# Ten of the twelve modulation vectors of a two-layer diffusion backbone are computed inside the attention stage, from raw fp32 weights

## The chip, the cores and the metric

The kernel runs on one core of a Trainium2 chip. Times are device microseconds of one execution. The kernel before took 2993.22 us, the median of three runs.

## What is computed

Two layers process 640 tokens of width 1024: 512 latent tokens and 128 context tokens. Each layer is modulated by six vectors of width 1024 (shift, scale and gate for each of its two halves), once for the latent and once for the context tokens, so there are 12 vectors of two rows each:

```python
mod_ctx = (silu(c_ctx) @ w_mod[l] + b_mod[l])          # w_mod[l]: 1024 x 6144, fp32
mod_lat = (silu(c) @ w_mod[l] + b_mod[l])
shift1, scale1, gate1, shift2, scale2, gate2 = split(mod, 6)
h = rms_norm(x, g_norm1) * (1 + scale1) + shift1
x = x + gate1 * token_mixing(h)                        # four mixers A, B, C, D, gates, output projection
h = rms_norm(x, g_norm2) * (1 + scale2) + shift2
x = x + gate2 * expert_choice_ffn(h)                   # 16 experts of 1024 x 1024 x 3
```

The results must agree with fp32 arithmetic closely enough for the router's choice of tokens, which is why all large products are made of three fp32r products (below).

## The kernel before, in words

It is written engine by engine, with semaphores and with the order of the work laid out by hand and by small planners at the top of the file.

**The ring.** SP (L502 to L608) fills a ring of weight chunks of 512 KB, in attention and in the modulation stage of 8 slots, in the expert stage of 16 (the slots beyond 8 lie over the attention's memory). ACT copies a chunk to `high` (fp32r, `split_high`, L1013), DVE makes `low` as the difference (`split_low`, L1325), and PE multiplies `high` and `low` (`three`, L464 to L468: high*high, low*high, high*low). `split_high` runs four chunks ahead of PE. A slot is refilled when PE has used its chunk (`ring_used`).

**The modulation stage** comes first. The 12 vectors (q = 0 to 11) are made one after another: 8 chunks of `w_mod` each (96 chunks, 50 MB), multiplied by the split pair of silu(c), silu(c_ctx) (`mod_rows`, L630), evacuated with the bias (`mod_evac`, L1364), high and low part summed by a small product with `pair_sum` (`mod_tail`, L646), evacuated with the gain (`mod_copy`, L1375) and stored in DRAM by ACT (`mod_store`, L1045). POOL loads the vectors from DRAM, broadcast to 128 partitions, where they are used (`mod_in`, L1783, and L1883, L1898, L1899). The first vectors' load (gain and shift of layer 0) is done while the stage still runs.

**A layer.** The norm (`stats`, L1399; PE turns it at L621), the projections of mixer D and of A (tiles of 128 tokens, all four chunks of a piece per tile, `dense_tile`), then the attention in 82 steps, one for each of 80 units (head, block of queries) and two to drain. In a step PE makes the scores of unit ui (L809), work of slot 0, the transposes of the probabilities of unit ui-1 (`turn`, L827), work of slot 1, the values of unit ui-2 (`values`, L837), work of slot 2. The work in the slots is written in the table `AT` by `plan_steps` (L128): the remaining projections (W), the gates (G) and the branch products (B), in pieces of one token tile by one chunk, and the transposes of the next heads. It fills PE between the steps of the softmax, in which DVE and ACT have their turns. After attention come the output projection, the second norm, the router, and 16 experts.

**Banks.** All work of the slots writes one of two PSUM banks, 5 and 7. `plan_uses` (L164) gives each use the bank that the use before it did not have, and while a tile is open (its four chunks not yet done) everything else goes to the other bank. `bank_free` (L682) lets PE wait until ACT or DVE has read what was in the bank before (`tile_out`, L1092, with L1101 for W and the tanh at L1109 for G; `gate_mul` for B, L1513).

## Time and profile before

| what | value |
|---|---|
| three runs | 2998.76, 2993.22, 2990.93 us |
| the profiled execution's own time | 2989.55 us |
| its span, first to last instruction | 2987.6 us |
| PE, DVE, ACT, POOL busy | 90%, 67%, 53%, 15% of the span |
| chain of work that ended last | PE 77%, DVE 10%, issue 5%, ACT 5%, DMA 2% |
| DMA | 593.80 MB, 199 GB/s on average |

The span falls into stages: modulation up to about 184 us, then for each layer norm and first projections, attention (285 to 868 us, and 1670 to 2256 us), output projection with norm and router, and experts. In a row of the profile an engine's busy time is that of its instructions. Matmuls overlap, so the spacing of their starts is the price of one, and the printed mean duration is more than that. A wait in brackets behind a row is the engine's idle time just before it, with what ended it. One fp32 matmul (not fp32r) leaves two records of MATMUL.

### The profile page before, as it was taken

Reading aid. Unit: us, or ns where it says so; the run is one execution under the profiler, and the core shown is the slowest. Engines: PE = TensorE matmul, PEld = TensorE weight load, DVE = VectorE, ACT = ScalarE, POOL = GpSimd, SP = SyncE. Lnnn points to the kernel's source line nnn. Section 1 sums busy time; section 2 is a strip of 40 time slices with the busy share of each in tenths; the row PEclk is TensorE's granted clock in tenths of the full one; section 3 lists DMA queues with packets and bytes.
Section 4 is the critical chain, followed back from the end, with each engine's and each line's share of the span. In section 5 each row is a group of like instructions: output and inputs, shape, how many; then the busy total and the mean of one; then the engine's idle time right before and its main releaser. Section 6 shows DMA issues by size and latency. Waiting matters only on the chain.

```text
span 2987.6 us, 40730 instructions
## 1 busy us (share of the span) xinstructions
PE 2686.8 (90%) x13616; PEld 1916.9 (64%) x13616; DVE 1987.8 (67%) x3069; ACT 1575.4 (53%) x2278; POOL 462.2 (15%) x335
## 2 busy tenths in 40 slices
PE   6779999999996699999988999999999499999994
PEld 1248777777775466666657777777777366666662
DVE  7864356535336799999975346643434699999994
ACT  5643344334323577777753444433422387777773
POOL 0003000212130112112211200031122112211201
PEclk8989999999998899999998999999999699999997
DMA  9942012112144699999983211121134399999994
GB/s 333 333 144 89 29 37 60 50 44 63 67 157 148 231 375 380 381 377 378 381 283 107 73 33 36 36 71 43 43 113 153 113 361 380 382 376 382 381 382 145
DMA packets 190521, 593.80 MB, mean 199 GB/s; under 512 B 22945, under 2 KB 32991, under 8 KB 190391
## 3 DMA queue, kind: packets, MB, share of 16 engines
q1 hardware_dynamic: 171638, 527.66, 48.0%
q0 software_dynamic: 18640, 64.20, 7.4%
q8 instruction: 79, 1.29, 0.2%
q14 instruction: 52, 0.42, 0.0%
q10 hardware_dynamic: 112, 0.23, 0.0%
HBM read 566.78 MB, written 25.23 MB: 198 GB/s over the span
## 4 chain that ended last, share of the span: by engine, by line
PE 77%; DVE 10%; issue 5%; ACT 5%; DMA 2%; ACTq 0%; SPq 0%; POOL 0%; DVEq 0%; POOLq 0%
PE bank L466 21%; PE bank L468 20%; PE bank L467 20%; PE bank L837 4%; PE bank L809 4%; DVE low L1329 2%; ACT high L1023 2%; PE bank L827 2%; PE bank L641 1%; PE bank L640 1%; DMA ring<-in_w_mod 1%; DVE st L1583 1%; PE bank L949 1%; PE bank L981 1%; DVE sigr L1513 1%
## 5 line engine op out<-in xcount | busy, mean ns | idle before, releaser
L1023 ACT ACTIVATE high<-ring 128x1024 fp32r<-128x1024 f32 (+1 forms) x1008 | 1053.8, 1052 | 447.0 <-PE bank L468 369.1
L1736 DVE TENSOR_TENSOR low<-ring,high 128x1024 fp32r<-128x1024 f32 x736 | 880.4, 1220 | 72.7 <-ACT high L1023 70.9
L466 PE MATMUL bank<-high,hT_high 128*128 128x512 f32 (+2 forms) x1280 | 520.9, 407 | 25.2 <-ACT sigr L1109 13.6
L467 PE MATMUL bank<-low,hT_high 128*128 128x512 f32 (+2 forms) x1280 | 485.4, 379 | 0.0
L468 PE MATMUL bank<-high,hT_low 128*128 128x512 f32 (+2 forms) x1280 | 484.2, 378 | 0.0
L1329 DVE TENSOR_TENSOR low<-ring,high 128x1024 fp32r<-128x1024 f32 (+2 forms) x272 | 321.8, 1210 | 138.7 <-ACT high L1023 137.7
L466 PE MATMUL bank<-high,xeT_high 128*80 128x512 f32 x1024 | 406.1, 397 | 2.1 <-DVE xeT_low L1334 2.1
L468 PE MATMUL bank<-high,xeT_low 128*80 128x512 f32 x1024 | 403.9, 394 | 0.0
L467 PE MATMUL bank<-low,xeT_high 128*80 128x512 f32 x1024 | 403.6, 394 | 0.0
L1210 ACT ACTIVATE att<-bank,st 128x640 f32<-128x640 f32 (+3 forms) x200 | 136.7, 684 | 351.2 <-DVE st L1588 256.5
L466 PEld LDWEIGHTS bank<-high,hT_high 128*128 128x128 f32 x1280 | 243.7, 190 | 78.4 <-ACT sigr L1109 18.2
L468 PEld LDWEIGHTS bank<-high,hT_low 128*128 128x128 f32 x1280 | 242.7, 190 | 47.4
L467 PEld LDWEIGHTS bank<-low,hT_high 128*128 128x128 f32 x1280 | 244.3, 191 | 32.5
L1583 DVE TENSOR_REDUCE st<-bank 128x1 f32<-128x640 f32 (+3 forms) x200 | 136.6, 683 | 116.6 <-PE bank L809 114.4
L466 PE MATMUL bank<-high,hidT_high 128*80 128x512 f32 x512 | 203.9, 398 | 10.6 <-DVE hidT_low L1334 8.9
L468 PEld LDWEIGHTS bank<-high,xeT_low 128*80 128x80 f32 x1024 | 151.8, 148 | 84.7 <-issue 0.7
L466 PEld LDWEIGHTS bank<-high,xeT_high 128*80 128x80 f32 x1024 | 151.9, 148 | 83.4 <-DVE xeT_low L1334 2.6
L467 PEld LDWEIGHTS bank<-low,xeT_high 128*80 128x80 f32 x1024 | 152.3, 149 | 80.4 <-issue 0.7
L468 PE MATMUL bank<-high,hidT_low 128*80 128x512 f32 x512 | 202.8, 396 | 0.0
L467 PE MATMUL bank<-low,hidT_high 128*80 128x512 f32 x512 | 202.7, 396 | 0.0
L1923 POOL DMA_INDIRECT x_resid<-oTr,idx_s x32 | 91.5, 2860 | 686.2 <-DVE oTr L1699 667.2
L1914 POOL DMA_INDIRECT U<-x_normed,idx_g x32 | 132.1, 4129 | 327.3 <-issue 104.2
(237 smaller groups left out, 3298.6 us busy)
## 6 DMA issues: line engine op xcount, KB each, us to landing
ring<-in_w_e_gate SPq DMA_DIRECT2D x256, 512.0 KB, 6.2
ring<-in_w_e_up SPq DMA_DIRECT2D x256, 512.0 KB, 6.9
ring<-in_w_e_down SPq DMA_DIRECT2D x256, 512.0 KB, 6.4
ring<-in_w_mod SPq DMA_DIRECT2D x96, 512.0 KB, 6.0
ring<-in_w_gate SPq DMA_DIRECT2D x64, 512.0 KB, 3.9
ring<-in_w_in SPq DMA_DIRECT2D x24, 512.0 KB, 4.5
ring<-in_w_branch SPq DMA_DIRECT2D x16, 512.0 KB, 4.2
ring<-in_w_out SPq DMA_DIRECT2D x16, 512.0 KB, 4.8
```

Source lines behind the costliest of these rows:

```text
L466: nc.tensor.matmul(out, lhs[0], rhs_high, start=start, stop=False)
L467: nc.tensor.matmul(out, lhs[0], rhs_low, start=False, stop=False)
L468: return nc.tensor.matmul(out, lhs[1], rhs_high, start=False, stop=stop)
L809: ins = mm(ps[p % 2][:, col:col + w], qT[r0:r0 + rn, b, un["m"] * P:(un["m"] + 1) * P], kT[r0:r0 + rn, b, a:a + w], start=True, stop=True)
L837: ins = mm(bank(6, P, P + HD), probT[:, ui % 2, i * P:(i + 1) * P], v_src(un, kb), start=(i == 0), stop=(i == len(un["kb"]) - 1))
L1023: A(high[:, HSLOT[g], :, 0:w], ring[:, SLOT[g], :, 0:w], ACT.Copy).then_inc(high_done, 1)
L1210: A(prob[:, p % 4, 0:w], ps[p % 2][:, 0:w], ACT.Exp, bias=negm[:, p % 8:p % 8 + 1], scale=SCALE[un["br"]], accum_out=sm[:, p % 8:p % 8 + 1 ...
L1329: V.tensor_tensor(low[:, SLOT[g], :, 0:w], ring[:, SLOT[g], :, 0:w], high[:, HSLOT[g], :, 0:w].bitcast(F32), ALU.subtract).then_inc(low_dv ...
L1583: then(V.tensor_reduce(mx[:, c8:c8 + 1], S[:, 0:w], AX.X, ALU.max))
L1736: V.tensor_tensor(low[:, SLOT[ahead], :, :], ring[:, SLOT[ahead], :, :], high[:, HSLOT[ahead], :, :].bitcast(F32), ALU.subtract).then_inc( ...
L1914: pool.indirect_dma_start(out=xe[0:CAP, b, :], out_offset=None, in_=xn_dram, in_offset=bass.IndirectOffsetOnAxis(ap=idx_g[:, b, 0:1], axis ...
L1923: pool.indirect_dma_start(out=x_dram, out_offset=bass.IndirectOffsetOnAxis(ap=idx_s[:, e, 0:1], axis=0), in_=ybuf[0:CAP, e, :], in_offset= ...
```

## The change

Only vectors 0 and 1 (shift and scale of layer 0's first half) are made in the modulation stage, now of 16 chunks. The other ten are made in attention, six in layer 0's and four in layer 1's. Each is cut into four quarters of 256 columns: 24 products in layer 0, 16 in layer 1. A product (`mod_product`) is eight fp32 matmuls on PE, silu(c) and silu(c_ctx) as two stationary columns and raw fp32 weights as the moving operand, no splitting. It stands in slot 1 of the steps 8 + 68*i//24 and takes a bank by the planner's rule. SP brings a quarter's weights (1 MB, four DMAs of 256 KB) into ring slots 6 and 7 once the product before it is done; attention's chunks have slots 0 to 5. ACT copies the two rows out of PSUM (`sum_out`), POOL stores them in DRAM; once a vector's quarters are there POOL loads it with the bias (and gain) as 64 partitions by 16 for either group, adds and multiplies, and stores it again (`raw_store`, `fin_load`, `fin_store`).

```diff
-N_MOD = 6 * D // NW
-CH_MOD = NQ * N_MOD * L
+RING_D = 6
+CH_MOD = 2 * KD
+MOD_COLS = 256
+MOD_ROWS = 2
+VECTORS = [[(0, 2), (0, 3), (0, 4), (0, 5), (1, 0), (1, 1)], [(1, 2), (1, 3), (1, 4), (1, 5)]]
+SUMS = [[(lv, v, a) for lv, v in vs for a in range(D // MOD_COLS)] for vs in VECTORS]
+SUM0 = [0, len(SUMS[0]), len(SUMS[0]) + len(SUMS[1])]
+N_PIECE = KD // MOD_ROWS
+def sum_step(i):
+    return 8 + 68 * i // len(SUMS[0])
...
     # plan_steps
+    for i in range(len(SUMS[0])):
+        at[sum_step(i)][1].append(("sum", i))
...
     # plan_uses
+        if x[0] == "sum":
+            freed[r] = ("sum", x[1])
+            continue
...
     # plan_ring
-        a, h = (SLOT_E[e % RING_E], e % HIGH_E) if e >= 0 else (g % RING, g % HIGH)
+        a, h = (SLOT_E[e % RING_E], e % HIGH_E) if e >= 0 else (g % RING if g < CH_MOD else (g - CH_MOD) % CH_LAYER % RING_D, g % HIGH)
...
+        mod_w = ring[:, RING_D:RING_D + 2, :, :].rearrange("p s h (k n) -> p (s h) k n", k=MOD_ROWS)
...
     # SP
+                mods = [(sum_step(i - 1) if i else -1, N_PIECE * (SUM0[l] + i) + k) for i in range(len(SUMS[l])) for k in range(N_PIECE)]
+                def mod_fills(step):
+                    while mods and mods[0][0] < step:
+                        nn = mods.pop(0)[1]
+                        i, k = divmod(nn, N_PIECE)
+                        lv, v, a = (SUMS[0] + SUMS[1])[i]
+                        if nn == N_PIECE * SUM0[l]:
+                            sp.wait_ge(ring_used, chunk_no(l, 0))
+                        if i and k == 0:
+                            sp.wait_ge(sum_full, i)
+                        src = w_mod[lv].rearrange("(k p) n -> p k n", p=P)[:, MOD_ROWS * k:MOD_ROWS * (k + 1),
+                                                                          v * D + a * MOD_COLS:v * D + (a + 1) * MOD_COLS]
+                        sp.dma_start(mod_w[:, k, :, :], src).then_inc(mod_w_in[k], 16)
...
                     for kq in range(chunks):
                         g = chunk_no(l, n)
+                        mod_fills(RELEASE_STEP[n])
                         fill(g, w_chunk(w, n0, width, kq), width)
...
     # PE
-            for q in range(L * 6):
+            for q in range(2):
                 mod_rows(q)
                 if q:
                     mod_tail(q - 1)
...
+                def mod_product(i):
+                    if i < len(SUMS[l]):
+                        n, r = SUM0[l] + i, USE["sum", i]
+                        bank_free(r)
+                        for k in range(KD):
+                            if k % MOD_ROWS == 0:
+                                pe.wait_ge(mod_w_in[k // MOD_ROWS], 16 * (n + 1))
+                            ins = mm(bank_use(r, 0, MOD_COLS)[0:2, :], csf[:, k, :], mod_w[:, k // MOD_ROWS, k % MOD_ROWS, :],
+                                     start=(k == 0), stop=(k == KD - 1))
+                        ins.then_inc(sum_full, 1)
...
     # ACT
-            for q in range(L * 6):
-                if q + 1 < L * 6:
-                    if q:
-                        act.wait_ge(mod_row, q)
-                    bias_in(q + 1)
...
+            bias_in(1)
+            for g in range(HIGH, CH_MOD + HIGH):
+                split_high(g)
+            for q in range(2):
                 mod_store(q)
...
+                def sum_out(i):
+                    if i < len(SUMS[l]):
+                        n = SUM0[l] + i
+                        act.wait_ge(sum_full, n + 1)
+                        if n:
+                            act.wait_ge(raw_out, 16 * n)
+                        A(mod_row2[:, :], bank_use(USE["sum", i], 0, MOD_COLS)[0:2, :], ACT.Copy).then_inc(sum_ev, 1)
...
     # POOL
+            def raw_store(i):
+                lv, v, a = (SUMS[0] + SUMS[1])[i]
+                pool.wait_ge(sum_ev, i + 1)
+                if i:
+                    pool.wait_ge(raw_out, 16 * i)
+                pool.dma_start(raw_dram[lv, :, v * D + a * MOD_COLS:v * D + (a + 1) * MOD_COLS], mod_row2[:, :]).then_inc(raw_out, 16)
...
+                for i in range(len(SUMS[l])):
+                    n = SUM0[l] + i
+                    mod_work.append((sum_step(i) + 1.5, raw_store, (n,)))
+                    if i % N_PIECE == N_PIECE - 1:
+                        mod_work.append((sum_step(i) + 2.5, fin_load, (VEC0[l] + i // N_PIECE, n)))
+                        mod_work.append((sum_step(i) + 3.5, fin_store, (VEC0[l] + i // N_PIECE,)))
```

**How the order moves, on SP.** These are SP's fills from the first attention chunks on, before:

```order
L516 DMA ring<-in_w_in 128x2x512 [waits ring_used] x4
L516 DMA ring<-in_w_gate 128x2x512 [waits ring_used] x4
L516 DMA ring<-in_w_branch 128x2x512 [waits ring_used]
L516 DMA ring<-in_w_gate 128x2x512 [waits ring_used] x4
L516 DMA ring<-in_w_branch 128x2x512 [waits ring_used]
```

and with the change, at the same place:

```order
L547 DMA ring<-in_w_in 128x2x512 [waits ring_used] x2
L603 DMA ring<-in_w_mod 128x2x256 [waits ring_used]
L603 DMA ring<-in_w_mod 128x2x256 x3
L547 DMA ring<-in_w_in 128x2x512 [waits ring_used] x2
L547 DMA ring<-in_w_gate 128x2x512 [waits ring_used] x2
L603 DMA ring<-in_w_mod 128x2x256 [waits sum_full]
L603 DMA ring<-in_w_mod 128x2x256 x3
L603 DMA ring<-in_w_mod 128x2x256 [waits sum_full]
L603 DMA ring<-in_w_mod 128x2x256 x3
```

SP now waits for products (`sum_full`) between the waits for chunks (`ring_used`), and four DMAs of raw weights stand behind each such wait.

**How the order moves, on PE.** This is layer 0's attention, step 42, where the first tile of mixer C's projection ends and the second begins. `bank2` holds bank 5, `bank3` bank 7; L837 are the values (in the other half of bank 6). Before:

```order
L837 MATMUL bank3<-U,att 128x64 x4
L466 MATMUL bank3<-high_51,hT_high 128x512
L467 MATMUL bank3<-low_50,hT_high 128x512
L468 MATMUL bank3<-high_51,hT_low 128x512
L466 MATMUL bank3<-high_51,hT_high 128x512
L467 MATMUL bank3<-low_50,hT_high 128x512
L468 MATMUL bank3<-high_51,hT_low 128x512
L466 MATMUL bank2<-high_51,hT_high 128x512
L467 MATMUL bank2<-low_50,hT_high 128x512
L468 MATMUL bank2<-high_51,hT_low 128x512
```

With the change:

```order
L918 MATMUL bank3<-ring_49,csf 2x256 x8
L893 MATMUL bank3<-att 128x64
L893 MATMUL bank3<-U,att 128x64 x4
L497 MATMUL bank2<-high_51,hT_high 128x512
L498 MATMUL bank2<-low_50,hT_high 128x512
L499 MATMUL bank2<-high_51,hT_low 128x512
L497 MATMUL bank2<-high_51,hT_high 128x512
L498 MATMUL bank2<-low_50,hT_high 128x512
L499 MATMUL bank2<-high_51,hT_low 128x512
L497 MATMUL bank2<-high_51,hT_high 128x512
L498 MATMUL bank2<-low_50,hT_high 128x512
L499 MATMUL bank2<-high_51,hT_low 128x512
```

Before, the second tile begins in the other bank; with the product (L918) inside the first tile, the second tile begins in the bank that the first has just left.

## Rows read from the trace of the kernel before

**Rows 1.** Busy time by stage (us, busy and count per engine, PEclk, DMA share, GB/s).

```profile
core 0: us, PE busy (x) PEld busy (x) DVE busy (x) ACT busy (x) POOL busy (x), PEclk, DMA share, GB/s
0.00:184.00 184.00, 134.20 (x428) 35.09 (x428) 143.97 (x148) 102.28 (x104) 5.07 (x13) 0.88 0.92 329
...
285.00:868.00 583.00, 549.55 (x3115) 440.81 (x3116) 273.27 (x656) 222.89 (x463) 73.77 (x61) 1.00 0.18 57
...
1670.00:2256.00 586.00, 553.52 (x3131) 443.84 (x3129) 274.99 (x658) 224.00 (x463) 74.71 (x61) 0.99 0.18 56
```

**Rows 2.** Timeline, PE and DVE at the end of vectors 1 and 11, norm.

```profile
28.99 0.62 PE L641 MATMUL bank<-high,csT 128*4 128x512 f32 x2
...
45.62 1.27 DVE L1371 TENSOR_TENSOR U<-bank,U 4x512 f32<-4x512 f32 x2
...
164.21 0.40 PE L641 MATMUL bank<-high,csT 128*4 128x512 f32 x1
...
183.59 1.27 DVE L1371 TENSOR_TENSOR U<-bank,U 4x512 f32<-4x512 f32 x2
...
188.52 1.28 DVE L1387 COPY U<-bank 2x512 f32<-2x512 f32 x2 [2.47 <-PE bank L652]
...
193.21 1.28 DVE L1418 SCALAR_TENSOR_TENSOR att<-att,st,M 128x1024 f32<-128x1024 f32 x1
```

**Rows 3.** Timeline, store of vector 1 by ACT, and POOL's load behind it.

```profile
61.14 0.24 ACTq L1048 DMA_DIRECT2D mod_rows<-U  x1
66.29 0.53 POOL L1787 DMA_DIRECT2D M<-mod_rows  x1 [56.08 <-DMA mod_rows<-U]
```

**Rows 4.** The same load's line: time to landing.

```profile
DMA to landing us min/median/max: 5.0/6.4/10.7
```

**Rows 5.** Timeline, PE, fp32 products before attention and in the modulation stage.

```profile
43.22 1.87 PE L652 MATMUL bank<-U,pair_sum 4*2 4x512 f32 x4
...
277.90 2.75 PE L760 MATMUL bank<-M 128*128 128x256 f32 x12
```

**Rows 6.** Timeline, PE, change from fp32 scores to fp32r chunks.

```profile
286.47 0.36 PE L466 MATMUL bank<-high,hT_high 128*128 128x256 f32 x1
286.67 0.28 PE L467 MATMUL bank<-low,hT_high 128*128 128x256 f32 x1
286.79 0.28 PE L468 MATMUL bank<-high,hT_low 128*128 128x256 f32 x1
```

**Rows 7.** What PE waited for, 285 to 868 us (first six of twelve).

```profile
PE bank L837 <- issue: 7.7, 11, 1.6
PE bank L466 <- ACT sigr L1109: 7.4, 8, 1.4
PE bank L809 <- ACT att L1178: 4.9, 8, 1.3
PE bank L809 <- ACT att L1175: 2.5, 2, 1.6
PE bank L851 <- DVE oT_low L1521: 2.5, 3, 1.6
PE bank L466 <- ACT U L1101: 2.4, 2, 1.7
```

**Rows 8.** Timeline, PE, tiles behind a tile in the same bank.

```profile
411.56 0.50 PE L466 MATMUL bank<-high,hT_high 128*128 128x512 f32 x1 [1.29 <-ACT sigr L1109]
443.91 0.50 PE L466 MATMUL bank<-high,hT_high 128*128 128x512 f32 x1 [1.41 <-ACT sigr L1109]
698.09 0.50 PE L466 MATMUL bank<-high,hT_high 128*128 128x512 f32 x1 [1.00 <-ACT sigr L1109]
```

**Rows 9.** Timeline, PE, a values group that waited in a step that gets a product.

```profile
352.26 0.96 PE L837 MATMUL bank<-M,att 128*128 128x64 f32 x7 [0.43 <-issue]
```

**Rows 10.** DMA issues: KB each, median us to landing.

```profile
ring<-in_w_in SPq DMA_DIRECT2D x24, 512.0 KB, 4.5
ring<-in_w_in SPq DMA_DIRECT2D x16, 256.0 KB, 3.2
```

**Rows 11.** The page's costliest groups: busy, mean ns, idle before.

```profile
L1023 ACT ACTIVATE high<-ring 128x1024 fp32r<-128x1024 f32 (+1 forms) x1008 | 1053.8, 1052 | 447.0 <-PE bank L468 369.1
...
L1329 DVE TENSOR_TENSOR low<-ring,high 128x1024 fp32r<-128x1024 f32 (+2 forms) x272 | 321.8, 1210 | 138.7 <-ACT high L1023 137.7
```

**Rows 12.** Timeline, PE in the modulation stage behind a wait, and without one.

```profile
36.81 0.58 PE L640 MATMUL bank<-low,csT 128*2 128x512 f32 x1 [2.78 <-DVE low L1329]
37.20 0.63 PE L641 MATMUL bank<-high,csT 128*4 128x512 f32 x1
37.62 0.63 PE L640 MATMUL bank<-low,csT 128*2 128x512 f32 x1
...
160.34 0.39 PE L641 MATMUL bank<-high,csT 128*4 128x512 f32 x1
160.57 0.40 PE L640 MATMUL bank<-low,csT 128*2 128x512 f32 x1
```

**Rows 13.** Timeline, POOL, mixer C's rotation and its wait in the middle.

```profile
559.05 1.27 POOL L1774 TENSOR_TENSOR U<-U,rope 128x192 f32<-128x192 f32 x2 [161.61 <-PE bank L851]
...
570.77 1.61 POOL L1843 DMA_DIRECT2D att<-rpb_padded  x2 [8.29 <-DVE st L1588]
```

More of the change, by code:

```diff
@@ L205 @@
 USE, USE_BANK, BEFORE, FREED, FULL, N_USE, LOWS_AFTER, LOWS_END = plan_uses()
+STEP_OF = {x: i for i, step in enumerate(AT) for slot in step for x in slot}
+RELEASE_STEP = [-1] * RING_D + [STEP_OF.get(("dense", pc, T - 1, kq), -1 if pc[0] == "W" else 2 * N_UNIT)
+                                for pc in STREAM for kq in range(CHUNKS_IN[pc])] + [2 * N_UNIT] * (2 * NQ)
 def count_of(*key):
@@ L269, in hybrid_step @@
         mod_dram = nc.dram_tensor("mod_rows", (L, 2, 6 * D), F32, kind="Internal").ap()
+        raw_dram = nc.dram_tensor("mod_raw", (L, 2, 6 * D), F32, kind="Internal").ap()
         rpb_dram = nc.dram_tensor("rpb_padded", (L, HEADS * 15, 127), F32, kind="Internal").ap()
@@ L398, in hybrid_step @@
         g_row_in = sem("g_row_in")
+        mod_w_in = [sem(f"mod_w_in{i}") for i in range(N_PIECE)]
+        sum_full, sum_ev, raw_out = sem("sum_full"), sem("sum_ev"), sem("raw_out")
+        fin_in, fin_out = sem("fin_in"), sem("fin_out")
         eps_set, sq_done = sem("eps_set"), sem("sq_done")
@@ L585, in matrix @@
                             sp.wait_ge(o_ev, N_UNIT * (l + 1))
+                        if i is None and SLOT[g + k] == RING_D:
+                            sp.wait_ge(raw_out, 16 * SUM0[l + 1])
                         if i is None and SLOT[g + k] == 13:
@@ L658, in _ @@
                     mod_tail(q - 1)
-            mod_tail(L * 6 - 1)
-            pe.wait_ge(sum_ready, L * 6)
+            mod_tail(1)
+            pe.wait_ge(sum_ready, 2)
             for l in range(L):
@@ L682, in bank_free @@
                 def bank_free(r):
-                    if BEFORE[r] is not None:
-                        by, n = FREED[BEFORE[r]]
-                        if by == "act":
+                    r = BEFORE[r]
+                    while r is not None and FREED[r][0] == "sum" and FREED[r][1] >= len(SUMS[l]):
+                        r = BEFORE[r]
+                    if r is not None:
+                        by, n = FREED[r]
+                        if by == "sum":
+                            pe.wait_ge(sum_ev, SUM0[l] + n + 1)
+                        elif by == "act":
                             pe.wait_ge(tile_act, N_USE["act"] * l + n)
@@ L857, in between @@
                             dense(*x)
+                        elif what == "sum":
+                            mod_product(*x)
                         elif what == "prep":
@@ L1053, in _ @@
                 split_high(g)
-            for q in range(L * 6):
-                if q + 1 < L * 6:
-                    if q:
-                        act.wait_ge(mod_row, q)
-                    bias_in(q + 1)
-                if q >= 2:
-                    mod_store(q - 2)
-                if q % 3 == 0 and q:
-                    gain_row_in(q + 1)
-                for k in range(KD):
-                    split_high(KD * q + k + HIGH)
-            for q in range(L * 6 - 2, L * 6):
+            bias_in(1)
+            for g in range(HIGH, CH_MOD + HIGH):
+                split_high(g)
+            for q in range(2):
                 mod_store(q)
@@ L1193, in between @@
                             prep_out(*x)
+                        elif what == "sum":
+                            sum_out(*x)
                         elif what == "oT":
                             turn_o_high(*x)
-                        elif x[0] == 2:
+                        elif what == "on" and x[0] == 2:
                             act.wait_ge(on_var, l + 1)
@@ L1391, in _ @@
                 split_low(g)
-            for q in range(L * 6):
+            for q in range(2):
                 for k in range(KD):
@@ L1804, in _ @@
                         mod_in(q1, g)
-                    for b in range(2):
-                        pool.wait_ge(mod_out[b], 16 * 3 * L)
                 def rope_rows(X, t0, tmp, heads, d4):
@@ L1819, in tile_done, with mod_until @@
                     pool.wait_ge(tile_act, N_USE["act"] * l + count_of("dense", pc, m))
+                mod_work = []
+                for i in range(len(SUMS[l])):
[4 more added lines that the diff above has]
+                        mod_work.append((sum_step(i) + 3.5, fin_store, (VEC0[l] + i // N_PIECE,)))
+                mod_work.sort(key=lambda w: w[0])
+                def mod_until(step):
+                    while mod_work and mod_work[0][0] < step:
+                        _, work, args = mod_work.pop(0)
+                        work(*args)
                 flat = lambda t: t[0, l].rearrange("t h n -> t (h n)")
```

50 lines of the change are left out of this document (43 added, 7 removed).

## The prediction

> **What bounds the kernel now.** I read the busy time by stage first, because a change that moves work from one stage to another is worth the difference of two prices. In the modulation stage (the first 184 us) the DMA engines are busy 0.92 of the time, while PE works 134 of 184 us; in both attention stages it is the other way round: DMA 0.18, PE 550 of 583 us and 554 of 586 us [rows 1]. So the stage that is shortened is bound by weights coming in (and by their splitting), and the stage that receives the work is bound by PE. Next I read the timeline around the ends of vectors, to see what a vector costs and what follows the last one [rows 2 to 4]; then the spacing of fp32 records, the price of a product [rows 5]; then what PE waits for in attention, to see how much room there is [rows 7].
>
> **The sum, part by part.** It is made against the profiled execution (2989.55 us, span 2987.6 us), which lies 3.7 us under the median of the three runs, 2993.2 us; differences are added to that median.
>
> *The modulation stage gets shorter.* Before, the last bias addition (vector 11) starts at 183.59 us and the norm's first multiplication at 193.21 us [rows 2]. With the change the order at the end of the stage is the same (last chunk of `w_mod`, 17 small loads, four chunks for mixer D whose lows DVE makes before it evacuates the last vector), only that the last fill is that of chunk 15. It waits for chunk 7's product: PE ends it at about 29.3 us instead of 164.6 us for chunk 87 [rows 2]. From there to the last evacuation took 183.59 - 164.6 = 19.0 us, so now 48.3 us. From the evacuation to the end of the last copy it is 189.8 - 183.6 = 6.2 us [rows 2]: 54.5 us. Now comes something that was hidden before: the norm needs gain and shift, which POOL loads only when both vectors are stored. ACT issued that store at 61.14 us, and POOL saw it at 66.29 us: 5.1 us, with the DMA engines full [rows 3]; they are empty now, so 3 to 5 us. The load itself takes 5.0 us at least and 6.4 us at the median [rows 4], behind a second issue of 0.5 us [rows 3]. Sum: 54.5 + 4 + 0.5 + 5.7 = 64.7 us, against 193.2: **-128.5 us** (bounds -125 and -131).
>
> *The products.* The nearest rows are the fp32 products of 256 columns before attention: 12 records in 2.75 us, of which some 0.17 us is the last one's tail, hence 0.213 us each; and four records of 512 columns over two stationary columns in 1.87 us, 0.427 us each [rows 5]. So width of the stationary side does not matter, and 0.213 us is the price. A product has 8 matmuls, 16 records: 3.41 us. 40 of them: **+136.5 us**, and PE has nothing better to do in their place only where it waits. *By the Trainium skill ("TensorE: Matmul & The Clock Gate", section on the back-to-back issue gap) a stream of load and matmul pairs sustains about 81 ns for 128 columns and 131 ns for 512; between them, an estimate of 98 ns a pass for 256, and the products would be 125 us. The rows show 107 ns a pass, two to a record, and they decide.*
>
> *Changing over.* Behind fp32 work the first fp32r matmul of a chunk holds the second off by 0.20 us where the next ones follow by 0.12 us [rows 6]. One such change for each product: 40 x 0.08 = +3 us.
>
> *Banks.* A product inside an open tile takes the other bank, and the next tile then gets the bank that the open tile is just leaving, so PE must wait for ACT's reading; a product behind a closed tile can itself land on a bank not yet read. Walking through the two orders, I count nine places in layer 0 and nine in layer 1, net of one that goes, in which a use now stands directly behind the reader of its bank. Such a place costs PE 1.0 to 1.4 us [rows 8], less where other work lies between: 1.0 us each, **+18 us**. Bounds: nothing, where ACT reads at once and scores lie between, and 18 x 1.4 = 25 us.
>
> *Waits that the products fill.* PE's visible idle time in attention is 583 - 550 = 33 us and 32 us [rows 1]. Only waits in the product's own step shrink. The product stands between turn and values, so the values no longer wait for ACT's copy of the transposes: 0.43 us in such a step [rows 9], four such steps a layer. The waits for ACT's sigmoid and exponentials in the list [rows 7] stand mostly in other steps, or are of the kind that the bank rule makes. I take -3 us a layer, **-6 us**; bounds: none, and a third of all idle time, -22 us.
>
> *Six ring slots instead of eight.* The third and fourth chunk of a projection are now asked for only when the first two chunks of the piece before are used, in a stretch where all four are needed for the first tile. They take 3.2 us (256 KB) and 4.5 us (512 KB) to land [rows 10] and then 1.05 us on ACT and 1.2 us on DVE [rows 11]. Following the times of the first projections of A, that is 0.3 us for the query piece and 1.1 us for the key and value piece, in both layers, and up to 0.5 us in the output projection: **+4 us**; bounds 0 and 10. In attention itself two uses of chunks lie about 5.5 us apart, which covers 4.5 us.
>
> *At no cost.* ACT's 40 small copies: ACT is busy 223 of 583 us [rows 1]; without that cover they would cost PE the bank time above again. SP's 160 DMAs: 1 MB per product over at least 16 us, on DMA engines that are busy 0.18. SP's new wait stands ahead of a chunk's fill, but always for a product of an earlier step than the release of that chunk's slot. POOL's 106 DMAs of about 0.53 us [rows 3] are 56 us on an engine that is busy 74 us of each 583. The expert stage reads 16 slots as before.
>
> Sum: -128.5 + 136.5 + 3 + 18 - 6 + 4 = **+27 us**, so 2993 + 27 = **3020 us**. The expected gain is there, and PE gives it back where it has no time to spare.
>
> **The rivals.**
>
> *A: PE's idle time swallows more.* If the products, wherever they stand, let ACT and DVE catch up so that a third of the 65 us of idle time goes, and the bank waits are covered too: -128.5 + 136.5 + 3 - 22 + 4 = -7, so **2986 us**, near no change. For it: most waits are short and of one kind, PE a little ahead of ACT [rows 7]. Against it: a wait behind a tile in the same bank comes back after each product, and the steps without a product (58 of 82 in layer 0) keep theirs.
>
> *B, the one on the other side: faster.* The mechanism is attention's slack: PE runs ahead until the softmax chain of a step (reduction, exponential, turn) is late, so a product in a step whose chain is later than PE costs nothing. It decides from the point where more than 17 us beyond the bank waits is swallowed. With two thirds of the idle time gone, -128.5 + 136.5 + 3 - 43 + 4 = -28: **2965 us**. Against it: idle time is only 6% of attention, and a step lasts some 7 us, of which the product takes half again.
>
> *C: POOL is late, and ACT with it.* ACT may copy a product's rows only when POOL has stored the ones before. In the middle of mixer B's first heads POOL is held by a wait for DVE of 8.3 us and then rotates mixer C's tiles [rows 13]; the store of the product of step 44 stands behind two of them. If ACT waits there, PE's next bank is late too: 3 to 10 us a layer on top, **3033 us**.
>
> *D: PE's clock falls.* In attention the granted clock is 1.00 [rows 1]. In the modulation stage it was lower: after a wait of 2.8 us, records of 512 columns stood 0.42 us apart (the 1.2 GHz level), in a stretch without such a wait 0.23 us (2.4 GHz) [rows 12]. What went before the fall was idle time, and the products bring none. If the clock did fall for each product, it would cost 3.4 us more apiece: 3020 + 136 = **3156 us**. [...]
>
> **How the numbers follow.** My forecast gets 0.62, A 0.20, B 0.06, C 0.09, D 0.03. A measurement of this kernel can tell about 0.3%, 9 us, from no change. A lies at -7 and spreads to both sides of that bound: 0.03 faster, 0.15 the same, 0.02 slower. The forecast's own range, from its bounds, is 3004 to 3040, with 0.02 in the band. So faster 0.09, same 0.17, slower 0.74. The range takes in most of A and C: 2988 to 3042 us leaves out B, D and the ends of A and C, some 0.2.
>
> **What the changed profile should show.** The norm's first multiplication (L1418 before) at 65 us. Products as groups of 16 records of 3.6 us with the tail, PEclk 1.00 around them. Attention 583 us before, some 673 us in layer 0, and 586 us before, some 648 us in layer 1. More waits of PE for ACT's sigmoid, about 8 us a layer. Nearly no wait of PE for the raw weights. Wrong would be: attention longer by clearly less than 3.4 us per product (A or B), ACT waiting for a DMA of POOL (C), PEclk under 0.95 in attention (D), or a start of the norm beyond 70 us.

## The result, and the profile after

The changed kernel takes 3031.8 us (median of 4 runs, 3029.3 to 3034.3) against 2994.7 us for the kernel before on the same chip: ratio 1.0124, 95% interval 1.0106 to 1.0141. It is slower by 37 us; 27 us were forecast. The profiled execution took 3034.3 us with a span of 3032.5 us, 44.9 us above the span of before (2987.6 us); the two profiles lie at opposite ends of their runs. Each variant below was timed beside the kernel before, not all of them on one chip, so two variants are compared by their ratios to it; a single profile can lie 8 us from the median of its kernel's runs.

First the busy time by stage, the answer to [rows 1] (us, busy time and count per engine, PEclk, DMA share, GB/s):

```profile
core 0: us, PE busy (x) PEld busy (x) DVE busy (x) ACT busy (x) POOL busy (x), PEclk, DMA share, GB/s
0.00:155.80 155.80, 114.17 (x536) 81.26 (x536) 82.02 (x149) 62.33 (x110) 26.98 (x50) 0.88 0.45 154
155.80:841.50 685.70, 647.58 (x3501) 476.83 (x3502) 274.23 (x656) 231.82 (x485) 108.47 (x137) 0.98 0.27 84
...
1648.00:2298.50 650.50, 613.36 (x3373) 463.22 (x3374) 274.40 (x656) 228.70 (x477) 96.46 (x111) 0.99 0.24 75
```

The three windows shown end at the first scores of layer 0, at the first transposes behind its attention, and at the end of layer 1's attention; the third begins at layer 1's first scores. Read in the same way, the stages moved so (us; the middle row is what lies between the two attentions, the last what follows the second):

| stage | before | after | difference | forecast |
|---|---|---|---|---|
| start to first scores | 285.4 | 155.8 | -129.6 | -128.5 and a part of the ring's +4 |
| attention, layer 0 | 583.2 | 685.7 | +102.5 | +90 |
| to the first scores of layer 1 | 800.5 | 806.5 | +6.0 | part of the ring's +4 |
| attention, layer 1 | 585.2 | 650.5 | +65.3 | +62 |
| the rest | 733.3 | 734.0 | +0.7 | 0 |

PE is busy for almost all of attention, as before; its idle time there is 38.1 and 37.1 us (33.5 and 32.5 us in [rows 1]). So most of what was added is PE's own work, and most of the excess over the forecast lies in layer 0. The clock is 0.98 there, not 1.00 (0.99 in layer 1).

The end of the modulation stage on the timeline, the answer to [rows 2, 3]:

```profile
47.89 1.27 DVE L1444 TENSOR_TENSOR U<-bank,U 4x512 f32<-4x512 f32 x2
...
50.39 3.98 ACTq L1118 DMA_DIRECT2D mod_rows<-U  x2
...
56.02 0.53 POOL L1896 DMA_DIRECT2D M<-mod_rows  x1 [46.32 <-DMA mod_rows<-U]
...
61.77 1.28 DVE L1492 SCALAR_TENSOR_TENSOR att<-att,st,M 128x1024 f32<-128x1024 f32 x1 [4.28 <-DMA oTr<-mod_rows]
```

The last bias addition stands at 47.89 us (48.3 forecast), and the norm's first multiplication at 61.8 us (64.7 forecast), now behind the load of gain and shift. Next one product in the stream, the answer to [rows 5, 6]:

```profile
198.13 0.71 PE L883 MATMUL bank<-ident,att 128*128 128x128 f32 x5
198.77 3.62 PE L918 MATMUL bank<-ring,csf 128*2 128x256 f32 x16
202.31 1.33 PE L893 MATMUL bank<-M,att 128*128 128x64 f32 x10
```

From the first of the 16 records to the next work it is 3.54 us, so 0.22 us a record with the change to the next work. All 40 products take 3.54 or 3.55 us: the term was 3.41 + 0.08 = 3.49 us.

### The profile page after: what moved, and what is told of

Same layout as the page of the kernel before. It is cut to its first block, busy times and chain, and to the rows that moved or that the text cites. A ratio compares the mean times of both kernels' runs of the same rounds, so it can differ in the third digit from the quotient of the medians.

```text
span 3032.5 us, 41346 instructions
## 1 busy us (share of the span) xinstructions
PE 2739.3 (90%) x13896; PEld 1946.5 (64%) x13896; DVE 1872.3 (62%) x2949; ACT 1511.2 (50%) x2238; POOL 508.2 (17%) x457
## 4 chain that ended last, share of the span: by engine, by line
PE 79%; DVE 7%; issue 5%; ACT 5%; DMA 4%; SPq 0%; POOL 0%; ACTq 0%; DVEq 0%; POOLq 0%
PE bank L497 21%; PE bank L499 19%; PE bank L498 19%; PE bank L918 5%; PE bank L893 4%; PE bank L865 4%; PE bank L883 2%; ACT high L1093 2%; DVE low L1402 1%; DMA ring<-in_w_gate 1%; DVE st L1657 1%; PE bank L672 1%; PE bank L1019 1%; DMA ring<-in_w_in 1%; PE bank L1051 1%
## 5 line engine op out<-in xcount | busy, mean ns | idle before, releaser
L1093 ACT ACTIVATE high<-ring 128x1024 fp32r<-128x1024 f32 (+1 forms) x928 | 974.2, 1052 | 425.7 <-PE bank L499 371.9
L1402 DVE TENSOR_TENSOR low<-ring,high 128x1024 fp32r<-128x1024 f32 (+2 forms) x192 | 229.0, 1206 | 127.2 <-ACT high L1093 126.4
L1682 DVE TENSOR_SCALAR U<-bank,st 128x64 f32<-128x64 f32 x120 | 34.1, 284 | 324.1 <-PE bank L893 323.3
```

Of the source, the lines that this page charges most:

```text
L1093: A(high[:, HSLOT[g], :, 0:w], ring[:, SLOT[g], :, 0:w], ACT.Copy).then_inc(high_done, 1)
L1402: V.tensor_tensor(low[:, SLOT[g], :, 0:w], ring[:, SLOT[g], :, 0:w], high[:, HSLOT[g], :, 0:w].bitcast(F32), ALU.subtract).then_inc(low_dv ...
```

## Where the unforeseen time sits

What PE waited for in layer 0's attention, and below it what ACT waited for from there to the end of the output projection (line, what it waited for, us in total, times, longest):

```profile
PE bank L497 <- ACT sigr L1171: 10.5, 10, 2.2
PE bank L865 <- ACT att L1240: 4.7, 8, 1.3
PE bank L893 <- issue: 4.2, 6, 1.5
PE bank L497 <- ACT U L1163: 3.1, 3, 1.7
...
PE bank L497 <- ACT att L1237: 2.7, 1, 2.7
...
PE bank L918 <- ACT sigr L1171: 1.4, 2, 0.7
PE bank L918 <- DVE sigr L1587: 1.1, 1, 1.1
PE bank L918 <- ACT U L1163: 0.9, 1, 0.9
```

```profile
ACT high L1093 <- DMA ring<-in_w_gate: 7.2, 5, 3.6
ACT high L1093 <- DMA ring<-in_w_out: 4.5, 4, 1.3
ACT mod_row L1250 <- DMA mod_raw<-mod_row: 3.2, 1, 3.2
ACT high L1093 <- DMA ring<-in_w_in: 1.1, 1, 1.1
```

Before the change ACT waited for no chunk of the ring in these stretches. Now it does, 12.8 us in layer 0 and 11.7 us in layer 1, more than half of it for gate weights; in the projections just ahead of the first scores it waits another 3.5 and 3.0 us. The longest such wait of layer 0 on ACT's timeline, and what PE made of it (in layer 1 it is 4.8 us on ACT and 3.4 us on PE):

```profile
792.51 1.06 ACT L1093 ACTIVATE high<-ring 128x1024 fp32r<-128x1024 f32 x1 [0.33 <-PE bank L499]
797.14 1.06 ACT L1093 ACTIVATE high<-ring 128x1024 fp32r<-128x1024 f32 x1 [3.58 <-DMA ring<-in_w_gate]
798.11 0.58 ACT L1171 ACTIVATE sigr<-bank 128x512 f32<-128x512 f32 x1
```

```profile
796.17 0.40 PE L499 MATMUL bank<-high,oT_low 128*128 128x512 f32 x1
798.74 0.57 PE L497 MATMUL bank<-high,oT_high 128*128 128x512 f32 x1 [2.17 <-ACT sigr L1171]
799.11 0.63 PE L498 MATMUL bank<-low,oT_high 128*128 128x512 f32 x1
799.53 0.63 PE L499 MATMUL bank<-high,oT_low 128*128 128x512 f32 x1
```

The wait is booked to ACT's sigmoid (L1171), because that came last. But ACT had stood idle for a transfer ahead of the split in front of that sigmoid; the line that a wait names is not its cause. A weight is asked for when the slot six chunks back is free; in the ring of eight it was asked for two chunks earlier. Behind the wait PE's records stand 0.43 us apart instead of 0.23 us until 802.5 us: the 1.2 GHz level. Five such stretches lie in layer 0: up to 160.7 us, and from 277, 287, 694 and 799 us, where before there was one (0.89 in a window of 15 us). The first three stand behind waits that the kernel before has too (1.26 us at 275.5 us, for example), the last two behind late chunks. The first three last some 12 us together, and records at that level stand about twice as far apart, so by estimate they cost 6 us, and the one before cost 2 us; why the clock fell there in this profile is not shown. In windows of 15 us, columns as above:

```profile
275.00:290.00 15.00, 12.99 (x72) 10.15 (x73) 10.79 (x24) 7.77 (x16) 1.15 (x2) 0.79 0.60 193
680.00:695.00 15.00, 11.62 (x60) 9.01 (x61) 5.90 (x12) 8.27 (x17) 2.70 (x2) 0.94 0.61 210
695.00:710.00 15.00, 14.14 (x61) 9.40 (x60) 7.23 (x15) 3.21 (x8) 6.21 (x5) 0.83 0.11 36
```

The stretch from 694 us stands behind the other late chunk: ACT stood 2.58 us for a gate chunk until 691.58 us and only then split it and made the copy for which PE waited 2.70 us.

Theory R: the ring of six slots, sized at 4 us, costs several times that, directly and through the clock. Rivals: S, the sum's sizes hold and the excess is the banks' (which the sum has at 18 us); P, it is something in the products themselves.

## The experiments

**The ring alone.** The kernel before, with this edit only:

```diff
+RING_D = 6
-        a, h = (...) if e >= 0 else (g % RING, g % HIGH)
+        a, h = (...) if e >= 0 else (g % RING if g < CH_MOD else (g - CH_MOD) % CH_LAYER % RING_D, g % HIGH)
```

> The kernel before, with only the dense stage's ring cut from 8 slots to 6 (no products in attention, the modulation stage of twelve vectors as it was). Theory R: the ring is what the prediction sized wrongly. Chunks asked for two slots later arrive late, ACT waits for them (some 13 us a layer in the changed kernel, none before), PE behind it, and its clock falls after the two longest of these waits: +20 to +28 us, about 3019 us. Theory S, the prediction's term: +4 us, about 2999 us. Theory P: the missing 10 us lie in the products and the banks, then this kernel is within 9 us of the one before and its ACT shows few waits for ring transfers.

Measured: 3005.5 us, ratio 1.0040 (1.0025 to 1.0055), so +12 us (7.5 to 16.5). Less than the 20 us of theory R; S's 4 us lie under the interval, and P, which had few waits for transfers, is contradicted by the timeline. The same late chunks of the last gates appear without any product (PE waits 2.51 us in layer 0, 3.56 us in layer 1; 0.57 us before). ACT and then PE, layer 0:

```profile
833.66 1.06 ACT L1024 ACTIVATE high<-ring 128x1024 fp32r<-128x1024 f32 x1 [3.92 <-DMA ring<-in_w_gate]
834.62 0.58 ACT L1110 ACTIVATE sigr<-bank 128x512 f32<-128x512 f32 x1
```

```profile
835.25 0.79 PE L467 MATMUL bank<-high,oT_high 128*128 128x512 f32 x1 [2.51 <-ACT sigr L1110]
835.85 0.63 PE L468 MATMUL bank<-low,oT_high 128*128 128x512 f32 x1
836.27 0.63 PE L469 MATMUL bank<-high,oT_low 128*128 128x512 f32 x1
```

Not all of it lies there. Against the profile of before, the two attentions are 6.4 and 2.9 us longer, the time to the first scores 2.9 us, and what lies between the attentions 5.7 us. That last stretch was not traced: products_alone, with eight slots, adds 1.5 us there, early_products, which gives its slots back before the stretch and takes two again at the start of layer 1, 5.6 us.

**The products alone.** The changed kernel with eight slots and a constant table in place of the raw weights, which are not loaded (so its ten vectors are not those of the computation):

```diff
-RING_D = 6
+RING_D = 8
-                        mod_fills(RELEASE_STEP[n])
-                            ins = mm(bank_use(r, 0, MOD_COLS)[0:2, :], csf[:, k, :], mod_w[...], ...)
+                            ins = mm(bank_use(r, 0, MOD_COLS)[0:2, :], csf[:, k, :], rope[...][:, 0:MOD_COLS], ...)
```

> The changed kernel with a ring of 8 slots and no transfer of raw weights: the 40 products stand where they stood, with their 16 records, but multiply a constant table of the same width, so the ten vectors are not those of the reference. Theory R: the two slots' price goes, 3032 - 25 = 3007 us (3002 to 3012), and ACT waits for no ring chunk in attention. Theory S (ring worth 4 us): 3028 us. Theory P as S.

Measured: 3017.1 us, ratio 1.0081 (1.0064 to 1.0098). The price of the two slots inside the change is the difference of the ratios, 0.0043 or 13 us, with some 7 us of uncertainty: again three times the term, and again half of R's size. Its stages:

```profile
154.70:828.40 673.70, 637.85 (x3501) 469.02 (x3502) 273.31 (x656) 231.47 (x485) 108.99 (x135) 1.00 0.16 49
...
1630.40:2278.30 647.90, 613.44 (x3374) 463.14 (x3375) 274.01 (x656) 228.84 (x477) 97.04 (x109) 0.99 0.17 51
```

Attention is 90.5 us and 62.7 us longer than before, where the forecast's steps for products, changing over, banks and filled waits gave 90 and 62. ACT waits for no ring chunk in either layer from the first scores to the end of the output projection, and PEclk is 1.00 and 0.99. P is out. In layer 0's attention this profile is 12.0 us shorter than that of the change, but half of that can be the three stretches of lower clock that stood behind no late chunk; the 13 us rest on the medians.

**Products early, the ring given back.**

```diff
 def sum_step(i):
-    return 8 + 68 * i // len(SUMS[0])
+    return 8 + i
+GROW = 30
+        if c == GROW:
+            free = [6, 7] + free
```

> The changed kernel with one product in each step from step 8 on (24 steps in layer 0, 16 in layer 1), and the ring back at 8 slots from chunk 30 of the layer on, once the last product is made. Everything is computed. Theory R: the late chunks of gates 4 to 7 and of the output projection come early again, three quarters of the ring's 25 us go: 3013 us (3008 to 3020). Theory S: 3030 us, no change that can be told. A third, C: with a product in every step POOL's stores of raw rows hold ACT up (one such wait of 3.2 us a layer in the changed kernel) and 3 to 10 us a layer come back: 3025 us or more.

Measured: 3017.4 us, ratio 1.0083 (1.0065 to 1.0101), as if the ring were whole, though everything is computed. ACT's waits for gate and output weights are gone in both layers (0.4 and 0.9 us of waits for `w_in` are left of 12.8 and 11.7 us), and C did not appear: ACT waits for no store of POOL. So most of the ring's price is paid by the chunks of the second half, as the timeline said; that the products' own places moved too was not separated.

**Products at tile edges.** Each product moved to the next place where a tile begins.

```diff
-        at[sum_step(i)][1].append(("sum", i))
+        s, j, k = min(... for ... if (s, j) >= (want, 1) and x[0] == "dense" and x[3] == 0)
+        at[s][j].insert(k, ("sum", i))
```

> The changed kernel with each product moved by up to two and a half steps so that it stands between two tiles instead of inside an open one; ring, transfers and number of products as in the change. The tile behind it then finds its bank's reader done 3.5 us earlier. The bank term of the prediction was +18 us; the traces of the changed kernel show the waits for ACT's and DVE's reading of tiles only 8 us longer in both layers together. If those 8 us go and nothing else changes: 3032 - 8 = 3024 us (3020 to 3028). If the bank order costs more than its visible waits (with the clock that falls behind them): 3014 to 3020 us. If it costs nothing (the waits only moved): 3032 us.

Measured: 3044.0 us, ratio 1.0153 (1.0134 to 1.0172): 9 us slower than the change, with some 8 us of uncertainty, which no theory expected. It does not speak on the banks, since the move ran into something else. ACT, and PE behind it:

```profile
499.52 0.37 ACT L1257 ACTIVATE mod_row<-bank 2x256 f32<-2x256 f32 x1 [17.98 <-DMA mod_raw<-mod_row]
```

```profile
499.94 0.80 PE L504 MATMUL bank<-high,hT_high 128*128 128x512 f32 x1 [6.32 <-ACT mod_row L1257]
500.54 0.63 PE L505 MATMUL bank<-low,hT_high 128*128 128x512 f32 x1
```

This is rival C of the prediction, at its place: POOL waited 11.8 us for DVE, rotated a tile of mixer C, and only then stored the rows that ACT's copy was waiting for; the same again in layer 1 (6.54 us on PE). In the changed kernel that wait is there too, 3.2 and 3.1 us of ACT, and PE does not feel it.

**The banks, without that.** The order is changed in two ways: the tile behind a product takes the product's bank, and each product is moved by at most a step and a slot.

```diff
-            at[r] = 1 - at[r - 1] if open_at is None and r else (1 - open_at if r else 0)
+            at[r] = 1 - turn_at if open_at is None and r else (1 - open_at if r else 0)
+            if x[0] != "sum" or open_at is None:
+                turn_at = at[r]
```

> The changed kernel with two edits in the order alone: the tile behind a product that stood inside an open tile takes the product's bank, not the one that is just being left; and each product is moved by up to a step and a slot to where its own bank has been read for 1.5 us. By the order, the places where a use stands directly behind the reader of its bank fall from 32 and 36 (layer 0, layer 1) to 24 and 22, as before the change (24 and 24). Ring, transfers, number and price of the products stay. If the bank term is what the waits of the changed kernel show, 8 us: 3024 us (3020 to 3028). If it is the prediction's 18 us: 3014 us. If bank waits only move (as at_tile_edges, which mixed them with a wait for POOL's stores, could not exclude): 3032 us.

Measured: 3019.9 us, ratio 1.0075 (1.0062 to 1.0088). Against the change that is 0.0049, 15 us, with some 7 us of uncertainty; 8 us and 18 us are both inside. Its stages:

```profile
154.85:828.50 673.65, 638.45 (x3501) 472.33 (x3502) 273.83 (x656) 232.49 (x485) 110.82 (x137) 0.99 0.27 86
1632.90:2276.20 643.30, 610.24 (x3374) 463.46 (x3375) 274.25 (x656) 229.48 (x477) 98.48 (x111) 0.99 0.24 76
```

Attention is 12.0 and 7.2 us shorter than in the change, though ACT waits for gate chunks as long as there (14.0 and 13.8 us over the run). Of these 19 us, 7 are idle time of PE and 12 are busy time, at a slightly higher clock; but this profile is the fastest of its five runs and that of the change the slowest of its four, and two low stretches of the change behind waits of before are not in it. That bank waits cost more than they show as waits (some 8 us in both layers), by the clock behind them, is therefore likely and not shown; the term of 18 us is neither confirmed nor refined.

**Both cures.** early_products with the banks edit and its own table of places.

> early_products with the edits of banks_kept: one product in each step from step 8 on, the ring back at 8 slots behind the last, the tile behind a product in the product's bank, each product at the best slot of its step. Everything is computed, all 16 records of a product stay. Theory: the ring's price (15 us by early_products) and the banks' (12 us by banks_kept) are separate: 3032 - 27 = 3005 us (3000 to 3010), so the products alone keep the kernel slower than before. Rival: with a product in every step the places behind a reader stay 31 and 32, against 24 before, and the gain of banks_kept does not come: 3014 to 3018 us.

Measured: 3031.5 us, ratio 1.0121 (1.0102 to 1.014): by the ratios 11 us slower than early_products alone, with some 8 us of uncertainty, and both the sum and the rival missed. The waits for banks did go (5.5 + 4.1 us ahead of products and tiles up to 480 us in early_products, here 1.4 us), but the places were less than a step apart in parts, and four products of layer 0 wait for their weights, for example

```profile
304.96 5.30 PE L942 MATMUL bank<-ring,csf 128*2 128x256 f32 x16 [2.12 <-DMA ring<-in_w_mod]
```

9.7 us together, and three more in layer 1, 7.1 us; behind each wait the product runs at the lower clock for a part: these rows show 5.3 to 6.4 us where others show 3.6. Whether the two cures add when spaced well was not tried.

**The weighting on DVE.** What is left of the excess is the price of 16 records. Here DVE multiplies and adds the eight rows for both vectors, and PE only adds over the partitions (4 records), with the ring whole again from chunk 54:

```diff
-                        for k in range(KD):
-                            ... mm(bank_use(r, 0, MOD_COLS)[0:2, :], csf[:, k, :], mod_w[...])
+                        pe.wait_ge(acc_done, 2 * KD * (n + 1))
+                        for g in range(2):
+                            ... mm(bank_use(r, 0, MOD_COLS)[0:2, :], sel[:, g, :], acc[:, g, :])
+    # DVE
+                            V.scalar_tensor_tensor(out=acc[:, g, :], in0=raw, scalar=c1, in1=acc[:, g, :],
+                                                   op0=ALU.mult, op1=ALU.add).then_inc(acc_done, 1)
```

> The products' weighting moved to DVE: DVE multiplies and adds the eight 256-column rows of a product for both conditioning vectors (16 operations of 128x256), and PE only adds over the partitions with two matmuls, 4 records for 16. Ring back at 8 slots from chunk 54 on. Everything is computed. If PE's time in the stream is what the products cost (theory R): 40 x 12 x 0.213 = 102 us less, and some 15 us of the ring: 3032 - 117 = 2915 us. Rival: DVE becomes late. By its rows (128x128 0.29 us, 128x512 0.69 us) an operation takes 0.42 us, 6.7 us a product, 161 us in layer 0's attention on top of 274 us, and if each of the 72 steps that get some waits 1 us longer for the softmax chain, half of the gain is eaten in both layers: 2915 + 60 = 2975 us or more.

Measured: 3017.7 us, ratio 1.0080 (1.0062 to 1.0099). The rival, and more: it is no faster than the variants that keep all 16 records. PE was busy 605.5 of 676.8 us in layer 0's attention, 71 us idle, at PEclk 0.96. A third of DVE's operations stood ahead of the copy for the turn and a third ahead of the next maximum. So the next kernel had all of them right ahead of DVE's wait for the values (each product also stands up to one step later):

```diff
                         then(V.reciprocal(rinv[:, r:r + 1], sm[:, p:p + 1]))
+                        acc_ops(ui, 0)
                         dve.wait_ge(o_full, N_UNIT * l + v + 1)
```

> As sums_on_dve, but DVE's 16 operations of a product stand in one place of each step, right ahead of its wait for the values, where it sat idle 176 us in layer 0 of the changed kernel; before, a third stood ahead of the copy for the turn and a third ahead of the next step's maximum, and PE waited 71 us in layer 0's attention (37 us in early_products). Theory L (the late softmax chain ate the gain): most of these 34 us and the clock's 20 us go in layer 0, half as much in layer 1: 3017 - 60 = 2957 us, within 2950 to 2975. Rival: DVE's work as such is too much, wherever it stands: 3005 us or more.

Measured: 2992.0 us, ratio 0.9982 (0.9972 to 0.9992). By the ratios 29 us came from the place, half of what theory L gave, and not by its path: in layer 0's attention PE's idle time fell by 4 us only (71.3 to 67.3), its busy time by 15 us (605.5 to 590.4), with PEclk 0.98 in place of 0.96. Four more runs varied where the products stand.

> sums_on_dve_2 with the products at tile edges as in at_tile_edges. If the bank waits add up with the rest: 8 us less than sums_on_dve_2. Rival: the uneven distances (one to four steps between products, so 16 operations of 0.4 us in one step twice) cost that much again: no difference.

Measured: 3021.6 us, ratio 1.0074 (1.0055 to 1.0093), 28 us slower than sums_on_dve_2: worse than its rival. ACT's copy waits 25.8 us for stores of POOL over the run (up to 9.3 us at once, and PE 5.3 us behind one of them), as in at_tile_edges; what the uneven distances add was not separated.

> sums_on_dve_2 with the same two edits of the order (places chosen for a product of 1 us). In sums_on_dve_2 PE waits longest at these: six waits for ACT's reading ahead of products, 8.2 us in each layer, and 14.7 and 12.2 us ahead of tiles. Theory: bank waits go back to those before the change, some 9 us a layer less: 2992 - 18 = 2974 us (2968 to 2982), a version under the kernel before. Rival: DVE's lateness takes their place (PE waits 8 us a layer for its U and att already): 2985 us or more.

Measured: 2989.5 us, ratio 0.9972 (0.996 to 0.9985). The rival: 3 us less than sums_on_dve_2, within the noise. The waits named below took the place of the bank waits:

```profile
PE bank L541 <- ACT U L1207: 7.2, 2, 5.2
PE bank L963 <- DVE ring L1691: 5.7, 3, 2.9
```

> sums_on_dve_3 with all products in the middle slot of their step, behind the turn, where DVE's last operation for them is long done. In sums_on_dve_3 eight stood in the first slot, and PE waited 5.7 us for DVE's sums in layer 0. Theory: those waits and a part of the clock that fell behind them go: 2989 - 8 = 2981 us (2976 to 2986). Rival: no change, 2989 us.

Measured: 2958.2 us, ratio 0.9869 (0.9851 to 0.9887): **faster than the kernel before by 39 us** (34 to 45), and than the change by 76 us. The gain over sums_on_dve_3 is 31 us, not 8. The wait for DVE's sums is gone, and so is the 5.2 us behind POOL's store (1.1 us of ACT are left of it). Between the two profiles PE's idle time in the attentions fell by 13 us and its busy time by 17 us, at a higher granted clock (0.97 and 0.99, before 0.96 and 0.97); so more than half of the gain is the clock behind the waits by this reading, which no run isolates. Its stages, and a product with part of its sums:

```profile
156.40:802.30 645.90, 591.32 (x3213) 455.44 (x3214) 427.50 (x1040) 229.87 (x485) 112.64 (x137) 0.97 0.29 91
...
1607.90:2220.10 612.20, 569.41 (x3181) 446.11 (x3182) 371.63 (x912) 227.39 (x477) 101.75 (x111) 0.99 0.27 82
```

```profile
183.97 3.26 DVE L1691 SCALAR_TENSOR_TENSOR ring<-ring,csf 128x256 f32<-128x256 f32 x8
...
188.53 1.02 PE L963 MATMUL bank<-ring,sel 128*2 128x256 f32 x4
```

Eight operations take 3.26 us, 0.41 each, as estimated; DVE is busy 427 of 646 us. Both attentions are 62.7 and 27.0 us longer than before, against 102.5 and 65.3 us in the change, and the modulation stage gives 129 us.

> sums_on_dve_4 with no product between steps 42 and 47, where POOL rotates mixer C's tiles and its stores of raw rows come late; in sums_on_dve_3 PE waited 5.2 us (layer 0) and 4.6 us (layer 1) there for an ACT that stood behind such a store, at a clock that had then fallen. Theory (rival C of the prediction, in one place): 10 us less than sums_on_dve_4, some 2972 us. Rival: the same work of DVE packed into fewer steps ahead of it costs that again: no difference to sums_on_dve_4.

Measured: 2959.0 us, ratio 0.9879 (0.9863 to 0.9896): no difference to sums_on_dve_4, as the rival said, though perhaps not for its reason: the long wait had already gone with the places of sums_on_dve_4, so the detour had little left to save.

## Why the prediction was right, and where a size was off

The direction and the mechanism held: the stage bound by transfers gave 129.6 us, and PE gave it back in attention. The 10 us between 27 and 37 us are of the size that one term, the ring, was off; the terms for banks and filled waits agree only as a sum.

- **The modulation stage**, -128.5 us: -131.4 us by the norm's first multiplication, -129.6 us by the first scores. From the end of the last copy (52.82 + 1.28 = 54.1 us) to the norm it was 7.7 us, where 4 + 0.5 + 5.7 us had been put.
- **The products**, +136.5 and +3 us: 40 x 3.54 = 141.6 us, 2 us above. The row of fp32 products [rows 5] was the right price, also for two stationary columns; with the tail of 0.17 us it gives 0.215 us a record rather than the 0.213 us that was used, which is half of the 2 us. *The estimate by the rates that the Trainium skill states ("TensorE: Matmul & The Clock Gate", section on the back-to-back issue gap), 125 us, was 17 us under what this trace shows.*
- **Banks and filled waits**, +18 and -6 us. The values' waits fell from 7.7 and 7.0 us to 4.2 us in each layer, 3 us a layer as said. The waits for readers of tiles rose by some 3 and 4 us, not by 9 a layer (5.6 and 7.7 us with the waits behind late chunks); the edit that takes them away brought 15 us, with 7 us of uncertainty (banks_kept). In products_alone attention grew by what the four terms say together, to a microsecond in each layer, but that is the sum and not each term, and in part luck: PE's idle time rose by 2.8 and 2.0 us only, and the other 7 us of the 12 that banks and filled waits were given are busy time of PE beyond 40 x 3.54 us, which no run assigns.
- **Six ring slots**, +4 us, bounds 0 to 10. This is the term that was mis-sized: 12 us alone (ring6_alone, interval 7.5 to 16.5), 13 us in the change. The sentence that failed is "In attention itself two uses of chunks lie about 5.5 us apart, which covers 4.5 us". Its working looked at the projections ahead of attention (where PE waits 0.6 us a layer for lows in the change) and took an average inside it. In the steps where one piece ends and the next begins a chunk is asked for and wanted within about one transfer, three such transfers share the queues (DMA share 0.92 from 820 to 835 us in ring6_alone), and what landed in 4.5 us at the median comes 3.6 and 2.6 us late in layer 0 of the change. Ahead of one of them (the chunk at 691.6 us) SP had also issued four pieces of raw weights (2.0 us), which the prediction had listed under "At no cost". That the clock falls behind such a wait was in no term.
- **The clock**, 1.00 in the forecast's checks: 0.98 and 0.99 in the two attentions. Rival D was wrong as it was put (the products themselves run at 2.4 GHz, all 40 of them), but what it read from its row held: idle time went before the falls, and late chunks bring idle time.
- **At no cost:** PE never waited for raw weights in the change, as said. POOL's stores held ACT up 3.2 us once a layer without reaching PE (rival C); moved by a step they cost PE 6 us a layer.
- A and B are out: attention was longer by more than 3.4 us per product, not less. Idle time did not swallow the products.

The expectations of the study had two errors of their own: theory R gave the ring all that the other terms left over in one profile (20 to 28 us), while two profiles of one kernel can lie several us apart and the medians gave 12 and 13; and the three runs that moved products to save bank waits and met another wait (at_tile_edges, early_and_banks, sums_on_dve_edges) came out 20 to 38 us over what was expected. sums_on_dve_4 missed by 23 us the other way.

## What to carry to other kernels

Work that moves from a stage bound by transfers to one bound by PE gains only the difference of two prices, so price it in the receiving engine's records; here PE's price in attention (141.6 us) was above the whole gain (131 us), and only giving the weighting to an engine that stood waiting made a gain of it. A slot that is taken from a ring was paid here mostly where pieces change, not on the average: look for the shortest distance between asking for a chunk and using it, and give the slots back as soon as they are free. Put added work on an engine right ahead of that engine's own wait for the bottleneck, and not ahead of what the bottleneck waits for: the same 640 operations cost some 29 us less there.

## What the runs showed of the hardware

A wait of PE costs more than itself where the clock falls behind it, but its length alone does not tell. Behind 2.70 us of idle time that ended at 693.9 us in the change, PE stayed at the lower level until 700.0 us, which by estimate (records twice as far apart) takes another 3 us; behind 2.17 us at 798.7 us for 3.8 us, another 1.9 us. Behind 3.56 us in layer 1 of ring6_alone the next records were 0.23 us apart, and the fall came 1.5 us later:

```profile
2229.36 0.50 PE L467 MATMUL bank<-high,oT_high 128*128 128x512 f32 x1 [3.56 <-ACT sigr L1110]
2229.70 0.39 PE L468 MATMUL bank<-low,oT_high 128*128 128x512 f32 x1
...
2230.86 0.60 PE L467 MATMUL bank<-high,oT_high 128*128 128x512 f32 x1
```

*The Trainium skill ("TensorE: Matmul & The Clock Gate", section "Why this matters for your kernels") states that with thin matmuls the clock oscillates at every step of the contraction unless all steps are done before the next transfer.* The products stand that way here, eight matmuls in a row with their weights loaded, and the trace agrees: all 40 products of the change took 3.54 or 3.55 us, and a stretch with one in each of 24 steps ran at PEclk 1.00 in early_products.
